# A two-block transformer kernel on one core: halves of square sums folded before TensorE adds them, values computed ahead of transposes, the last layer along rows of tokens, and an earlier first table load

## The chip, the cores and the metric

The kernel runs on 1 core of a Trainium2 chip. The metric is the device time of one execution in microseconds (us). The engines named below are TensorE (PE; PEld is its weight load), VectorE (DVE), ScalarE (ACT), GpSimd (POOL) and SyncE (SP, which here only issues transfers).

## What is computed

256 tokens of width 1024 pass through two blocks, all in float32, with one output of 256 x 1024. Cut to the order of the work:

```
# first block, layer 0: 8 heads of neighbourhood attention + 8 heads of latent attention
x = x + even_mixer(rms_norm(x), ...)          # w_in 1024x1952, w_o 1024x1024
x = x + square(relu(rms_norm(x) @ w1)) @ w2   # 1024x4096, 4096x1024
# layer 1: dilated attention, 3 groups of 16 heads
x = x + odd_mixer(rms_norm(x), ...)           # w_in 1024x9216, w_o 1024x1024
x = x + square(relu(rms_norm(x) @ w1)) @ w2
x = rms_norm(x, norm_final)
# second block: LRU, block attention and attention over a memory, gated and merged
x = x + merged(rms_norm(x)) @ w_out
h = rms_norm(x)
g = causal_dwconv(h @ w_ffn_gate)             # 1024x3072
x = x + (gelu(g) * (h @ w_ffn_up)) @ w_ffn_down   # 3072x1024, "the last layer"
return rms_norm(x, final_norm_gain)
```

## The kernel before

Activations lie transposed: `XT` holds x with features on the partitions, 8 chunks (c) of 128 features by S = 256 tokens. A float32 product is made of three fp32r matmuls: each operand is split into a high and a low part (`XH`/`XL` of the activations, `whi`/`wlo` of the weights, `HH`/`HL` of a hidden layer), and high x high, low x high and high x low are added in PSUM (`product`, L515). Weights come as 192 slabs of at most 1 MB. SP loads slab n into `raw` (5 buffers), ACT makes `whi` (3 buffers, L975), DVE (L1357) or POOL (L2020) makes `wlo`. Each engine calls `ahead(n)` where its program wants slab n + 2 prepared; every engine runs its own program in written order, and waits are on semaphores (`once.wait_ge(*at(event))`). PSUM has 8 banks that TensorE takes in turn (`bank`); a bank is taken again only when its last use is `taken`.

Places that the change touches:

- **Sums of squares for the norms.** ACT squares two chunks at a time into a 128 x 512 tile, DVE or POOL adds the four squares (`add_square`, L1367 and L2031), and `sums` (L572, L576) lets TensorE add over the partitions with a matrix of ones, in true float32: one 256-wide matmul for each half of the tile, and where `cols` is asked for, one 1-wide matmul for each half and each 128 tokens as well. A true float32 matmul leaves two records in the trace.
- **Attention.** `attend(first, n, s)` is step s of a pipeline over heads (u): `scores` of a pair, `transposes` of head s - 2 (L656) and `values` of the pair that ends with head s - 3 (L685). In the first attention (19 steps over 16 heads) other work stands between the steps; in steps 5 to 8 the memory input of the second block is turned (`turn_in`, L587), ACT makes its high part (`memory_high`, L1115) and DVE its low part (`memory_low`, L1623), which also frees the PSUM bank of the turn. DVE's `memory_low(s - 6)` stands behind the whole of `attend`, whose last part is `outputs` (L1458), the low part of the pair's output.
- **Merging of the second block.** On ACT `branch(4)` and `branch(5)` prepare a weight slab each and then wait for merged values (L1271).
- **Last layer.** `down` multiplies with the weights as the stationary operand and 256 tokens as the moving one: 4 column blocks j, 3 slabs each, two halves m, so 576 matmuls of 256 columns. x comes out transposed, is scaled by the gain (`XG`), turned back by TensorE (`rows_out`, L940, 16 transposes), and scaled by the last norm's factor, for which TensorE adds the squares (L958).
- **Start.** SP loads the identity, the first gains, then x in four transfers. TensorE turns x (L587); ACT makes `XH` and `whi` (L1007, L1092); `first_features` (L535) is the first product.

Of the kernel before, what the change touches and what calls it, by code (L numbers as in the profile page):

```python
# [11 lines left out]
P = 128  # L12
S = 256
# [7 lines left out]
        ("ffng", 8), ("fin2", 8), ("qn", 2), ("kvn", 1), ("cw", 16), ("cb", 4), ("ba", 4), ("bx", 4),  # L21
# [104 lines left out]
def weight_plan(A):  # L126
# [67 lines left out]
    down("fd", A["w_ffn_down_2"][0], 24)  # L194
# [81 lines left out]
def build(nc, A, out):  # L276
    with ExitStack() as ctx:
# [21 lines left out]
        with nc.sbuf_tensor("BIG", [P, 16384], F32) as BIG:  # L299
# [35 lines left out]
        s_bias, s_half, s_mem, s_vec, s_roper, s_namask, s_lruw, s_out, s_ident, s_dmask, s_alibi, s_mix = (sem(n) for n in (  # L335
            "s_bias", "s_half", "s_mem", "s_vec", "s_roper", "s_namask", "s_lruw", "s_out", "s_ident", "s_dmask", "s_alibi", "s_mix"))
# [119 lines left out]
        XG, orow = big(14336, 2048, 8), big(6144, 2048, 2)  # L456
# [35 lines left out]
        def tensor(pe):  # L492
# [72 lines left out]
            def sums(name, slot, n=2, cols=False, dilated=False):  # L565
# [179 lines left out]
            def latent_kv():  # L745
# [3 lines left out]
                sums("nq", 1)  # L749

            def rotary_key():
# [4 lines left out]
                sums("nk", 1, n=1)  # L756
# [178 lines left out]
            def rows_out(j):  # L935
                b = bank(("rows", j))
                once.wait_ge(*at(("gained", j)))
                for t in range(2):
                    for c in range(2):
                        m = pe.transpose(b[:, t * S + c * P:t * S + c * P + P], XG[:, 2 * j + c, t * P:(t + 1) * P], ident[:, :])  # L940
                m.then_inc(*tell(s_product, ("product", "rows", j)))

            h = h_ready(2, 24)
            for j in range(4):
                b = [bank(("down", 2, j, m)) for m in range(2)]
                for s in range(3):
                    n = FD + 3 * j + s
                    for m in range(2):
                        event = ("product", "down", 2, j, m) if s == 2 else ("weights", n) if m else None
# [4 lines left out]
            b = bank(("last",))  # L954
            once.wait_ge(*at(("norm", "n7")))
            for t in range(2):
                for c in range(2):
                    m = pe.matmul(b[:, t:t + 1], acc(1)[:, c * S + t * P:c * S + t * P + P], ones[:, 0:1], start=c == 0, stop=c == 1)  # L958
            m.then_inc(*tell(s_product, ("product", "last")))
            rows_out(3)  # L960

        def scalar(act):
# [131 lines left out]

# [237 lines left out]
            for j in range(4):  # L1332
# [7 lines left out]
                if j:  # L1340
                    rows_out(j - 1)
# [897 lines left out]
```

## Time and profile before

| | us |
|---|---|
| median of 3 runs | 1265.96 (1265.52 to 1267.0) |
| profiled execution, its own time | 1267.13 |
| its span, first to last instruction | 1265.3 |
| PE busy | 1245.1 |
| DVE, ACT, POOL busy | 820.8, 618.7, 274.8 |

Busy time of PE includes the time in which a matmul runs through the array, so that PE can be shown as busy while it is issued less often than it could be; the distance between the starts of matmuls is the finer measure. The clock column PEclk is 1.00 at 2.4 GHz and 0.50 at 1.2 GHz.

### The profile page before, as it was taken

How to read it: one execution, taken by the hardware profiler on the slowest of the kernel's cores; microseconds unless marked ns; L12 is line 12 of the kernel's file. 1: busy time of each engine (PE TensorE's matmuls, PEld its weight loads, DVE VectorE, ACT ScalarE, POOL GpSimd, SP SyncE). 2: the span in 40 equal slices, each digit the busy share in tenths (PEclk: the TensorE clock that was granted, in tenths of full speed). 3: DMA queues.
4: the chain of work that ended last, by engine and by line, in shares of the span. 5: the costliest groups of instructions: out<-in, count | busy, mean ns of one | idle time of the engine just before them, and what ended most of it. 6: DMA issues, size and time to landing. Idle time of an engine off the chain costs nothing.

```text
span 1265.3 us, 23972 instructions
## 1 busy us (share of the span) xinstructions
PE 1245.1 (98%) x10309; PEld 1207.0 (95%) x10309; DVE 820.8 (65%) x1106; ACT 618.7 (49%) x765; POOL 274.8 (22%) x205
## 2 busy tenths in 40 slices
PE   7999999999999999999999999999999999999997
PEld 7968899999999999999999999999999999999997
DVE  6768666655565666666877655487876477665653
ACT  5565455544344454545555553345665445444441
POOL 2500010000021202020310000389211595444000
PEclk9999999999999999999999999999999999999998
DMA  9543356555576655464355655555553455555550
GB/s 262 185 134 101 106 170 191 177 189 176 191 225 204 188 170 181 150 191 151 101 166 171 196 171 195 170 172 173 170 165 134 163 170 168 187 180 188 179 167 34
DMA packets 194711, 214.00 MB, mean 169 GB/s; under 512 B 5235, under 2 KB 182718, under 8 KB 194606
## 3 DMA queue, kind: packets, MB, share of 16 engines
q1 hardware_dynamic: 189518, 204.93, 50.3%
q10 hardware_dynamic: 4896, 7.08, 2.0%
q8 instruction: 81, 1.33, 0.5%
q0 software_dynamic: 192, 0.46, 0.1%
q14 instruction: 24, 0.20, 0.1%
HBM read 205.11 MB, written 1.05 MB: 163 GB/s over the span
## 4 chain that ended last, share of the span: by engine, by line
PE 92%; DVE 3%; ACT 2%; POOL 1%; DMA 1%; issue 1%; ACTq 0%; SPq 0%; DVEq 0%; POOLq 0%
PE ps L515 79%; PE ps L648 3%; PE ps L551 3%; PE ps L685 2%; PE ps L656 2%; DVE wlo L1357 1%; PE ps L572 1%; PE ps L535 1%; DVE XL L1391 1%; POOL wlo L2020 1%; DMA TB<-TA 0%; ACT whi L975 0%; ACT SN L1037 0%; ACT XH L1007 0%; ACTq L1195 0%
## 5 line engine op out<-in xcount | busy, mean ns | idle before, releaser
L1357 DVE TENSOR_TENSOR wlo<-raw,whi 128x2048 fp32r<-128x2048 f32 (+1 forms) x155 | 360.1, 2326 | 202.1 <-ACT whi L975 202.0
L515 PE MATMUL ps<-XH,whi 128*128 128x256 f32 x1592 | 451.8, 285 | 0.0
L515 PE MATMUL ps<-XH,wlo 128*128 128x256 f32 x1592 | 448.3, 283 | 0.3 <-DVE wlo L1357 0.3
L515 PE MATMUL ps<-XL,whi 128*128 128x256 f32 x1592 | 448.0, 283 | 0.0
L975 ACT ACTIVATE whi<-raw 128x2048 fp32r<-128x2048 f32 (+1 forms) x189 | 359.5, 1905 | 176.6 <-PE ps L515 154.7
L515 PEld LDWEIGHTS ps<-XH,whi 128*128 128x128 f32 x1592 | 304.3, 192 | 3.2 <-issue 2.9
L515 PEld LDWEIGHTS ps<-XH,wlo 128*128 128x128 f32 x1592 | 304.3, 192 | 0.9 <-DVE wlo L1357 0.8
L515 PEld LDWEIGHTS ps<-XL,whi 128*128 128x128 f32 x1592 | 304.3, 192 | 0.0
L2020 POOL TENSOR_TENSOR wlo<-raw,whi 128x512 fp32r<-128x512 f32 x136 | 180.3, 1358 | 319.5 <-ACT whi L975 319.5
L515 PE MATMUL ps<-HH,whi 128*128 128x256 f32 x832 | 229.5, 283 | 0.0
L515 PE MATMUL ps<-HL,whi 128*128 128x256 f32 x832 | 229.3, 283 | 0.0
L515 PE MATMUL ps<-HH,wlo 128*128 128x256 f32 x800 | 226.5, 283 | 1.0 <-POOL wlo L2020 1.0
L515 PEld LDWEIGHTS ps<-HH,whi 128*128 128x128 f32 x832 | 157.5, 192 | 0.0
L515 PEld LDWEIGHTS ps<-HL,whi 128*128 128x128 f32 x832 | 157.5, 192 | 0.0
L515 PEld LDWEIGHTS ps<-HH,wlo 128*128 128x128 f32 x800 | 153.6, 192 | 1.2 <-POOL wlo L2020 1.2
L2083 POOL TENSOR_TENSOR TB<-TB,BIG 128x512 f32<-128x512 f32 x24 | 42.7, 1781 | 367.4 <-DMA TB<-TA 367.4
L1037 ACT ACTIVATE SN<-SN,stat 128x512 f32<-128x512 f32 (+2 forms) x64 | 38.2, 597 | 102.2 <-DVE stat L1425 93.2
L515 PE MATMUL ps<-whi,XH 128*128 128x256 f32 x256 | 73.2, 286 | 0.0
L515 PE MATMUL ps<-whi,XL 128*128 128x256 f32 x256 | 72.4, 283 | 0.0
L515 PE MATMUL ps<-wlo,XH 128*128 128x256 f32 x256 | 72.4, 283 | 0.0
L515 PE MATMUL ps<-OH,whi 128*128 128x256 f32 x192 | 56.3, 293 | 0.0
L1079 ACT ACTIVATE HH<-TB 128x512 fp32r<-128x512 f32 x32 | 20.2, 632 | 72.7 <-DVE TB L1513 72.7
(229 smaller groups left out, 1604.0 us busy)
## 6 DMA issues: line engine op xcount, KB each, us to landing
raw<-in_mlp_w_dram SPq DMA_DIRECT2D x64, 1024.0 KB, 5.4
raw<-in_od_w_in_dram SPq DMA_DIRECT2D x36, 1024.0 KB, 5.4
raw<-in_w_in_dram SPq DMA_DIRECT2D x24, 1024.0 KB, 5.2
raw<-in_w_ffn_gate_dram SPq DMA_DIRECT2D x12, 1024.0 KB, 5.1
raw<-in_w_ffn_up_dram SPq DMA_DIRECT2D x12, 1024.0 KB, 5.1
raw<-in_w_ffn_down_dram SPq DMA_DIRECT2D x12, 1024.0 KB, 5.0
raw<-in_ev_w_in_dram SPq DMA_DIRECT2D x6, 1024.0 KB, 11.6
TB<-TA ACTq DMA_DIRECT2D x96, 64.0 KB, 4.1
```

The source lines that it names most:

```text
L515: m = pe.matmul(to, l[c][a], r[c][b], start=first and k == 0, stop=last and k == 3 * n - 1)
L535: i = pe.matmul(b[:, m * S:m * S + S], w[m][c][a], x[c][z], start=k == 0, stop=k == len(order) - 1)
L551: i = pe.matmul(b[n][:, m * S:m * S + S], h[a], x[c][z], start=m == c == a == z == 0, stop=m == 1 and c == 7 and z == 1)
L648: m = pe.matmul(banks[u][:, lo:hi], l, r, start=start, stop=stop)
L656: m = pe.transpose(b[:, to:to + P], SN[:, u % 3, of:of + P], ident[:, :])
L685: m = pe.matmul(b[p0:p0 + n, a:z], v, PT[:, u % 3, lo:hi], start=start, stop=stop)
L975: act.activation(whi_of(n), raw_of(n), ACT.Copy, scale=1.0).then_inc(*tell(s_whi, ("whi", n)))
L1037: m = act.activation(SN[:, u % 3, lo:hi], src[:, lo:hi], ACT.Exp, bias=stat[:, u % 3, k:k + 1], scale=-1.0 if biased else 1.0, accum_out=s ...
L1079: act.activation(HH[:, 512 * j:512 * j + 512], TB[j % 2][:, :], ACT.Copy, scale=1.0).then_inc(*tell(s_xhi, ("hhi", layer, j)))
L1357: dve.tensor_tensor(wlo_of(n), raw_of(n), f32(whi_of(n)), ALU.subtract).then_inc(*tell(s_wlo, ("wlo", n)))
L2020: m = pool.tensor_tensor(lo[:, v], r[:, v], f32(hi[:, v]), ALU.subtract)
L2083: pool.tensor_tensor(z, z, twice(RP[:, S:512]), ALU.mult).then_inc(*tell(s_pool, ("sine", k)))
```

## The change

- `sums` gets one half: the adding engine first folds the two halves of the tile (128 x 256 added to 128 x 256), and TensorE runs half the matmuls. For the sums before the last layer (`n6`) the 1-wide ones (`cols`) are added.
- In `attend` on TensorE, `values` stands before `transposes`, and on DVE `memory_low` stands before `outputs`.
- The last layer runs along rows of tokens: HH and HL are the stationary operand (128 features x 128 tokens), and 512 columns of the weights the moving one, 288 matmuls. x is turned to rows beforehand (`rows_in`, 16 transposes among the slabs of the layer before). The square sums then come from ACT's accumulator, along the free dimension. The last gain is loaded as a broadcast row.
- ACT issues the transfers of the identity and the first gains, and runs one Copy at once, which loads its table. TensorE gets 12 matmuls of ones with ones (`keep_busy`), around the turning of x.
- On ACT, the slab of `branch(5)` is prepared before the merged values are waited for.

```diff
@@ weight_plan
-    down("fd", A["w_ffn_down_2"][0], 24)
+    for half in range(2):
+        for k in range(6):
+            add("fd", A["w_ffn_down_2"][0], 4 * k * P, 4, 512 * half, 512)
@@ tensor
-            def sums(name, slot, n=2, cols=False, dilated=False):
+            def sums(name, slot, n=1, cols=False, dilated=False):
@@ attend
+                if 0 <= s - 3 < n and members(group_of(first + s - 3))[-1] == first + s - 3:
+                    values(group_of(first + s - 3))
                 if 0 <= s - 2 < n:
                     transposes(first + s - 2)
-                if 0 <= s - 3 < n and members(group_of(first + s - 3))[-1] == first + s - 3:
-                    values(group_of(first + s - 3))
@@ start
+            def keep_busy(n):
+                once.wait_ge(*at("ones"))
+                for _ in range(n):
+                    pe.matmul(ps[7][:, 0:P], ones[:, :], ones[:, :], start=True, stop=True)
+            keep_busy(3)
             ...
             pe.transpose(b[:, 0:16], rows_[0:16, 2, :], ident[0:16, 0:16])...
+            keep_busy(4)
             for c2 in range(4):
+                if c2 == 2:
+                    keep_busy(2)
                 turn_in(("x", c2), ...)
+            keep_busy(3)
@@ last layer
-            features(FF + 1, x, between=lambda: sums("n6", 0))
+            features(FF + 1, x, between=lambda: sums("n6", 0, cols=True))
             for n in range(FF + 2, FD):
                 features(n, x)
+                if n - FF in (4, 8, 12, 16):
+                    rows_in((n - FF - 4) // 4)
-                        product(b[m][:, 0:S], w_ready(n, 8, m * P, P), h[8 * s:8 * s + 8], event, first=s == 0, last=s == 2)
-                if j:
-                    rows_out(j - 1)
+            for q in range(2):
+                b = [bank(("down", 2, q, t)) for t in range(2)]
+                for k in range(6):
+                    n = FD + 6 * q + k
+                    for t in range(2):
+                        ht = [(HH[:, c * S + t * P:c * S + t * P + P], HL[:, ...], ...) for c in range(4 * k, 4 * k + 4)]
+                        product(b[t][:, :], ht, w_ready(n, 4, 0, 512), event, first=k == 0, last=k == 5)
@@ scalar
+            act.dma_start(ident[:, :], A["c_ident"])...
+            act.dma_start(rows_[0:16, 2, :], A["norm_mix"]...)...
+            once.wait_ge(*at("ones"))
+            act.activation(GG[:, 0:1], ones[:, 0:1], ACT.Copy, scale=1.0)
@@ scalar, last layer
+            def squared_rows(q, t):
+                once.wait_ge(*at(("xr", q, t)))
+                act.activation(..., XR[:, t, 512 * q:512 * q + 512], ACT.Square, accum_out=stat[:, t, q:q + 1])...
+            def row_root(t): ...   # Sqrt of 128 x 1
+            def scaled_row(t, q):
+                once.wait_ge(*at(("root", "n7", t)))
+                once.wait_ge(*at(("yr", q, t)))
+                v = YR[:, t, 512 * q:512 * q + 512]
+                act.activation(v, v, ACT.Copy, scale=r7[:, t:t + 1])...
+            act.dma_start(out[0, P:2 * P, 512:1024], YR[:, 1, 512:1024])...
@@ vector, add_square (gpsimd's alike)
+                if done:
+                    a = acc(slot)
+                    once.wait_ge(*at(("summed", norm, i)))
+                    dve.tensor_tensor(a[:, 0:S], a[:, 0:S], a[:, S:2 * S], ALU.add)...
@@ vector, first attention
-                attend(EVEN, 16, s)
+                attend(EVEN, 16, s, lambda: memory_low(s - 6) if 6 <= s < 10 else None)
-                if 6 <= s < 10:
-                    memory_low(s - 6)
@@ vector, last layer
+            def row_sums(q, t):
+                b = take(("down", 2, q, t), [("taken", "rows", 2 * q + 1)])
+                v = slice(512 * q, 512 * q + 512)
+                dve.scalar_tensor_tensor(out=XR[:, t, v], in0=b[:, :], scalar=r6c[:, t:t + 1], in1=XR[:, t, v], op0=ALU.mult, op1=ALU.add)...
+                dve.tensor_tensor(YR[:, t, v], XR[:, t, v], G2[:, v], ALU.mult)...
+            for t in range(2):
+                row_sums(1, t)
+                row_mean(t)
+                row_scale(t)
@@ sync
-            sp.dma_start(ident[:, :], A["c_ident"])...
-            sp.dma_start(rows_[0:16, 2, :], A["norm_mix"]...)...
```

Three places of the programs are shown as rows, each the instructions of one engine in order. DVE in step 6 of the first attention, from the last maximum (L1425, L1459) on: OL is the output's low part, HL the low part of the memory, SN and PT the probabilities. Before:

```order
L1425 ISA SN,stat<-ps,BIG 128x256
L1425 ISA stat 128x1
L1458 TENSOR_TENSOR OL<-ps,OH 128x256
L1623 SCALAR_TENSOR_TENSOR HL<-ps,V,HL 128x256 x2
L1437 RECIPROCAL stat<-stat 128x2
```

and with the change:

```order
L1459 ISA SN,stat<-ps,BIG 128x256
L1459 ISA stat 128x1
L1657 SCALAR_TENSOR_TENSOR HL<-ps,V,HL 128x256 x2
L1492 TENSOR_TENSOR OL<-ps,OH 128x256
L1471 RECIPROCAL stat<-stat 128x2
```

The low part of the memory now stands ahead of the output's low part, so it no longer waits for ACT's OH; nothing else on DVE has moved here.

TensorE in step 8 of the same attention: scores (L648, L653), the transposes of the probabilities (L656, L661), the values (L685, L690) and the last turn of the memory (MK and MV hold its rows). Before:

```order
L648 MATMUL ps<-BIG 128x256 x8
L656 MATMUL ps<-ident,SN 128x128 x4
L685 MATMUL ps<-PT,BIG 64x256 x4
L587 MATMUL ps<-ident,MK 128x128
L587 MATMUL ps<-ident,MV 128x128
```

and with the change:

```order
L653 MATMUL ps<-BIG 128x256 x8
L690 MATMUL ps<-PT,BIG 64x256 x4
L661 MATMUL ps<-ident,SN 128x128 x4
L592 MATMUL ps<-ident,MK 128x128
L592 MATMUL ps<-ident,MV 128x128
```

The values have moved ahead of the transposes of the next heads; the same happens in every step that has both.

ACT at the end of the merging, in steps 13 and 14 of the third attention: OH is the last head's output, `whi` a weight slab, HH the high part of the merged values. Before:

```order
L1055 ACTIVATE OH<-ps 128x256
L975 ACTIVATE whi<-raw 128x2048
L1271 ACTIVATE HH<-BIG 128x512 x2
L975 ACTIVATE whi<-raw 128x2048
L1271 ACTIVATE HH<-BIG 128x512 x2
```

and with the change:

```order
L1065 ACTIVATE OH<-ps 128x256
L985 ACTIVATE whi<-raw 128x2048 x2
L1285 ACTIVATE HH<-BIG 128x512 x4
L985 ACTIVATE whi<-raw 128x2048 x3
```

The second slab stands ahead of the first two high parts instead of behind them.

## Rows read from the trace of the kernel before

**Rows 1.** The page, busy time: engine, us (share of the span), instructions
```profile
PE 1245.1 (98%) x10309; PEld 1207.0 (95%) x10309; DVE 820.8 (65%) x1106; ACT 618.7 (49%) x765; POOL 274.8 (22%) x205
```

**Rows 2.** TensorE's waits: engine line, whom for, us in total, times, longest
```profile
PE ps L648 <- DVE HL L1623: 2.2, 1, 2.2
PE ps L515 <- POOL wlo L2020: 1.0, 1, 1.0
```

**Rows 3.** Two stretches: length, busy PE, PEld, DVE, ACT, POOL, then PEclk, DMA, GB/s
```profile
87.00:89.40 2.40, 0.23 (x3) 0.00 (x0) 1.23 (x4) 2.40 (x8) 0.00 (x0) 1.00 0.04 14
89.80:96.40 6.60, 6.60 (x28) 2.99 (x24) 4.48 (x13) 2.48 (x9) 0.00 (x0) 0.50 0.01 2
```

**Rows 4.** The first attention in order of time: start, us, engine, line
```profile
84.12 0.60 ACT L991 ACTIVATE SQ<-ps 128x512 f32<-128x512 f32 x1
85.73 0.18 ACT L1037 ACTIVATION_READ_ACCUMULATOR SN<-SN,stat 128x1 f32 x1
...
87.78 0.36 ACT L1055 ACTIVATE OH<-ps 128x256 fp32r<-128x256 f32 x1
88.52 0.87 DVE L1623 SCALAR_TENSOR_TENSOR HL<-ps,V,HL 128x256 fp32r<-128x256 f32 x2
89.44 4.46 PE L648 MATMUL ps<-BIG 64*128 64x256 f32 x16 [2.20 <-DVE HL L1623]
90.75 0.68 DVE L1448 COPY PT<-ps 128x512 f32<-128x512 f32 x1
```

**Rows 5.** TensorE and POOL at the merging's end, in order of time
```profile
1018.80 1.90 ACT L975 ACTIVATE whi<-raw 128x2048 fp32r<-128x2048 f32 x1
1020.84 6.42 POOL L2020 TENSOR_TENSOR wlo<-raw,whi 128x512 fp32r<-128x512 f32 x4 [3.16 <-ACT whi L975]
```

**Rows 6.** The start in order of time
```profile
1.63 1.84 SPq L2152 DMA_DIRECT2D BIG<-in_x_dram  x4
7.14 1.28 ACT L1007 ACT_TABLE_LOAD   x1 [7.14 <-DVE XT L1543]
13.02 1.83 PE L535 MATMUL ps<-XL,whi 128*128 128x256 f32 x8
14.14 1.92 ACT L975 ACTIVATE whi<-raw 128x2048 fp32r<-128x2048 f32 x1 [0.33 <-DMA raw<-in_ev_w_in_dram]
16.60 2.08 PE L535 MATMUL ps<-XH,wlo 128*128 128x256 f32 x16
23.02 2.29 DVE L1357 TENSOR_TENSOR wlo<-raw,whi 128x2048 fp32r<-128x2048 f32 x1 [1.18 <-ACT whi L975]
```

**Rows 7.** Float32 matmuls of 256 and of 512 columns, in order of time
```profile
79.06 1.89 PE L785 MATMUL ps<-BIG 128*128 128x256 f32 x8
80.79 1.88 PE L791 MATMUL ps<-raw,BIG 128*128 128x512 f32 x4
```

**Rows 8.** The sums n4 and n5, in order of time
```profile
826.37 1.02 PE L572 MATMUL ps<-SQ,ones 128*128 128x256 f32 x4
828.04 1.11 PE L572 MATMUL ps<-SQ,ones 128*128 128x256 f32 x4
```

**Rows 9.** The end in order of time
```profile
1254.20 0.60 PE L940 MATMUL ps<-ident,BIG 128*128 128x128 f32 x4
...
1254.40 0.42 DVE L1493 TENSOR_TENSOR TA<-ps,RS 128x256 f32<-128x256 f32 x1 [2.00 <-PE ps L515]
...
1255.32 0.63 ACT L991 ACTIVATE SQ<-XT 128x512 f32<-128x512 f32 x1 [14.79 <-DVE XT L1495]
...
1256.04 0.69 DVE L1367 TENSOR_TENSOR SQ<-SQ 128x512 f32<-128x512 f32 x1 [0.75 <-ACT SQ L991]
...
1258.76 0.20 ACT L1343 ACTIVATE RS<-RS 128x2 f32<-128x2 f32 x1 [2.33 <-DVE RS L1999]
...
1260.02 0.71 ACT L1347 ACTIVATE BIG<-BIG,RS 128x512 f32<-128x512 f32 x1
```

**Rows 10.** The four transfers of the output, from issue to landing
```profile
DMA to landing us min/median/max: 2.1/2.5/2.8
```

More of the change, by code:

```diff
@@ L930, in tensor, with rows_in @@
             features_by_chunks([FF], x)
-            features(FF + 1, x, between=lambda: sums("n6", 0))
+            features(FF + 1, x, between=lambda: sums("n6", 0, cols=True))
+            def rows_in(j):
+                b = bank(("rows", j))
+                for t in range(2):
+                    for c in range(2):
+                        m = pe.transpose(b[:, t * S + c * P:t * S + c * P + P], XT[:, 2 * j + c, t * P:(t + 1) * P], ident[:, :])
+                m.then_inc(*tell(s_product, ("product", "rows", j)))
@@ L954, in tensor @@
[L954 to L960, printed above, removed]
+                if n - FF in (4, 8, 12, 16):
[5 more added lines that the diff above has]
+                    for t in range(2):
+                        event = ("product", "down", 2, q, t) if k == 5 else ("weights", n) if t else None
+                        ht = [(HH[:, c * S + t * P:c * S + t * P + P], HL[:, c * S + t * P:c * S + t * P + P], ("hhi", 2, c // 2),
+                               ("hlo", 2, c // 2)) for c in range(4 * k, 4 * k + 4)]
+                        product(b[t][:, :], ht, w_ready(n, 4, 0, 512), event, first=k == 0, last=k == 5)
+                    released[n] = [event]
@@ L1325, in scalar @@
             ffn_high(11)
-            def rows_out(j):
-                b = take(("rows", j))
-                act.activation(orow[:, :, 256 * j:256 * j + 256], pair(b[:, :]), ACT.Copy, scale=1.0).then_inc(
-                    *tell(s_act_out, ("taken", "rows", j)))
-            for j in range(4):
-                for s in range(3):
-                    ahead(FD + 3 * j + s)
-                once.wait_ge(*at(("xt", "down", 2, j)))
-                if j == 0:
-                    once.wait_ge(*at("ones"))
-                    act.activation(GG[:, 0:1], ones[:, 0:1], ACT.Sqrt)
-                square("n7", 1, j, x0[j], ("xt", "down", 2, j))
-                if j:
-                    rows_out(j - 1)
@@ new lines, in scalar @@
+            for k in range(6):
+                ahead(FD + k)
+            once.wait_ge(*at("ones"))
+            act.activation(GG[:, 0:1], ones[:, 0:1], ACT.Sqrt)
+            for t in range(2):
+                squared_rows(0, t)
+            for k in range(6, 12):
+                ahead(FD + k)
+            for t in range(2):
+                squared_rows(1, t)
+                row_root(t)
+                scaled_row(t, 1)
+            once.wait_ge(*at(("row", 1, 1)))
+            act.dma_start(out[0, P:2 * P, 512:1024], YR[:, 1, 512:1024]).then_inc(*tell(s_out, ("out", 1), by=16))
@@ new lines, in row_mean, with row_scale @@
+            def row_mean(t):
+                once.wait_ge(*at(("rows squared", 1, t)))
+                dve.scalar_tensor_tensor(out=r7[:, t:t + 1], in0=stat[:, t, 1:2], scalar=1.0 / D, in1=stat[:, t, 2:3], op0=ALU.mult,
+                                         op1=ALU.add).then_inc(*tell(s_dve, ("mean", "n7", t)))
+            def row_scale(t):
+                once.wait_ge(*at(("sqrt", "n7", t)))
+                dve.reciprocal(r7[:, t:t + 1], r7[:, t:t + 1]).then_inc(*tell(s_dve, ("root", "n7", t)))
+                once.wait_ge(*at(("root", "n7", t)))
+                once.wait_ge(*at(("yr", 0, t)))
+                dve.tensor_scalar(YR[:, t, 0:512], YR[:, t, 0:512], r7[:, t:t + 1], None, ALU.mult).then_inc(*tell(s_dve, ("row", t, 0)))
@@ new lines, in vector @@
+            for k in range(6):
+                ahead(FD + k)
+            for t in range(2):
+                row_sums(0, t)
+            for t in range(2):
+                once.wait_ge(*at(("rows squared", 0, t)))
+                m = dve.tensor_scalar(stat[:, t, 2:3], stat[:, t, 0:1], 1.0 / D, EPS, ALU.mult, ALU.add)
+            m.then_inc(*tell(s_dve, "rows' first half"))
+            for k in range(6, 12):
+                ahead(FD + k)
+            once.wait_ge(*at("rows' first half"))
```

121 lines of the change are left out of this document (55 added, 66 removed).

## The prediction

> **What bounds the kernel now.** I read the page's busy times first: TensorE is busy for 1245.1 of 1265.3 us, the next engine for two thirds of that [rows 1]. So only two kinds of thing can move the time: TensorE getting less to do or doing it at a shorter distance, and the few places where it waits. The view of its waits names two in the middle, one of 2.2 us in the first attention and one of 1.0 us at the merging's end [rows 2]; the timeline of the start and of the end shows what lies around its work [rows 6, 9]. In the windows I looked for the clock: one stretch of the first attention runs at 0.50 although TensorE is busy all through [rows 3]. Six terms come out of this.
>
> **Term 1, the last layer's matmuls.** 16 fp32r matmuls of 256 columns took 2.08 us [rows 6]. The columns alone are 16 x 256 / 2.4 GHz = 1.71. Eight records of float32 ones of 256 columns took 1.89 and four of 512 took 1.88 [rows 7], so the time goes with the columns alone, at two cycles each: 8 x 256 x 2 / 2.4 GHz is 1.71 as well. So about 0.18 is the last one's way through the array, and the fp32r ones lose a further (2.08 - 1.71 - 0.18) / 15 = 0.013 each: they start 0.120 apart, the float32 ones 0.213 to 0.216. At 1.2 GHz eight fp32r ones of 256 columns took 1.83 [rows 6], and their columns alone are 1.71: nothing lost. The loss thus shows only where a matmul streams for no more than 0.107 us, and is gone in all rows where it streams for 0.213. With 512 columns of fp32r it streams for 0.213, and I take 0.216. 576 x 0.120 = 69.1 becomes 288 x 0.216 = 62.2, a gain of 6.9. The bounds are 0.213 (gain 7.7) and 0.240, where the loss would grow with the columns (gain 0). Against it stand four more turning transposes in TensorE's stream (16 where 12 stood ahead of the last product), at 0.60 for four with the way through the array [rows 9]: 0.4. Net 6.5. DVE's and ACT's work for a slab (2.29 and 1.9 [rows 5, 6]) still fits the 5.2 us of a slab.
>
> The Trainium skill, "TensorE: Matmul & The Clock Gate", section "Back-to-back issue gap", gives columns / 2.4 GHz + 2.5 ns for single matmuls. By that the 512-wide ones would start 0.216 apart, as I take it, and the 256-wide ones 0.109, which the trace contradicts with 0.120. The same section gives some 131 ns at 512 columns for a sustained stream with weight loads; no row here starts wide matmuls faster than their columns stream, and what that would do is a rival below.
>
> **Term 2, the end.** The last product ended at 1254.40, where DVE takes it [rows 9], and the span ends at 1265.3: 10.9. With the change the chain behind the last product is, each with its row's time for the same shape: DVE joins x and the product (0.69 as the 128 x 512 add), ACT squares with its sum (0.63 + 0.18 [rows 4, 9]), DVE a tiny one, ACT's tiny square root (0.20), DVE a tiny reciprocal (0.2 each), ACT scales 128 x 512 (0.71), then the transfer with 2.1 to 2.8 to land [rows 10], I take 2.5. Sum 0.69 + 0.81 + 0.6 + 0.71 + 2.5 = 5.3, and 0.5 for six handovers and for DVE coming late from the rows of the first 128 tokens, whose own chain (about 2.8) is just longer than the 2.6 us (12 x 0.216) of the last product: 5.8. Gain 5.1; bounds 4.5 and 5.6. DVE's multiplication with the gain lies beside ACT's squares.
>
> **Term 3, the first attention.** Before, step 8's scores waited until 89.44 for DVE's L1623 at 88.52, the low part of the memory, which frees their PSUM bank [rows 2, 4]. DVE was late there because it first waited for ACT's OH, done only at 88.14. Its inputs from ACT were ready when the squares ended at 84.72 [rows 4]. With the low part ahead of the output's, it can run at about 86 and the scores start when TensorE arrives, at 87.25. What is late next: the values, which now stand ahead of the transposes, need the probabilities that DVE copies at 90.75 to 91.43 [rows 4]. DVE keeps its order up to there except that 0.87 of work has moved into its wait, so this copy ends about 0.7 earlier, at 90.8. The scores would end at 89.3 at full clock, TensorE waits 1.5, does the values, then the transposes. Second effect: the wait of 2.2 was followed by 6.8 us at 0.50 clock [rows 3], in which the same sixteen scores took 4.46. With scores in the place of the wait and 1.5 as the longest pause, I expect the clock to stay up. That part is then worth 6.8 / 2 = 3.4, and the wait 2.2 - 1.5 = 0.7, less about 0.1 for handovers: gain 4.0. Bounds: 0.6, if the clock falls all the same, and 5.6 if no wait is left. Values ahead of transposes costs nothing elsewhere, since in other steps a slab of 5.8 us lies between a copy of probabilities and its use, and 0.5 here at most; without that slab as cover it costs the wait for one copy, 0.7.
>
> The Trainium skill, same page, section "Part 4: PE-mode transpose", says that transposes do not count as work for the clock. Ahead of the wait here TensorE had run turns and transposes alone, which agrees with a fall after a pause of only 2.2; no row separates the two.
>
> **Term 4, folded sums.** A full set with 1-wide matmuls takes 828.04 - 826.37 = 1.67 [rows 8]; half of it 0.83. The sums mem, n2, n4 and n5 are such: 3.3. n1 and n3 have the 256-wide ones alone, four records of 0.215, half of which is 0.43: 0.9 for both. n6 saves 0.43 and adds as much in 1-wide ones. Gain 4.2; nq and nk keep their work, and n0 is in the next term. The fold itself is a 128 x 256 add on DVE (under 0.69) or POOL, hidden behind the two products that stand ahead of each sum; if it came late, the nearest case is n5, whose add ends 1.5 before its use. Bounds 3.4 and 4.6.
>
> **Term 5, the merging's end.** POOL's slab of 6.42 started at 1020.84, after ACT's `whi` of 1018.80 to 1020.70, and TensorE waited 1.0 for it [rows 2, 5]. ACT can now make this slab when branch 4's product frees the buffer, some 4 us earlier, and POOL starts 3.16 earlier (its idle time). The wait goes. ACT's high parts come 1.9 later, and DVE behind them; the slack of the first is over 2 us. Gain 1.0; bounds 0 and 1.0.
>
> **Term 6, the start.** Four issues take 1.84 [rows 6], so two fewer ahead of x bring all of SP's transfers forward by 0.9. ACT waits for slab 1 at 14.14 and DVE's `wlo` of slab 2 at 23.02 hangs on ACT [rows 6]: this chain moves by 0.9. DVE's idle 1.18 there swallows the fold of n0. TensorE was about a microsecond later than DVE; the folded n0 gives back 0.8 of that. The table load of 1.28 leaves ACT's path, but the weights' transfers bound ACT next. The 12 matmuls of ones lie in waits and raise the clock before 13.02, where it was still low; this too ends at the same transfers. Gain 1.6; bounds 0.9 (transfers alone) and 2.5.
>
> **Sum.** 6.5 + 5.1 + 4.0 + 4.2 + 1.0 + 1.6 = 22.4. The profiled execution took 1267.1 with a span of 1265.3, so its like becomes 1244.7 with a span of 1242.9; the runs' median stands 1.2 below the profiled one, hence 1243.6.
>
> **Rivals.**
> - *All terms hold* (chance 0.60): 1243.6, own range 1241 to 1246.
> - *The clock still falls in the first attention* (0.16). For it: two pauses of 1 to 2 us remain near 89 and transposes stand around them [rows 3, 4]. Against: the pause is shorter and scores fill the old one. 1243.6 + 3.4 = 1247.0.
> - *The loss per matmul grows with the columns* (0.12), 0.240 for 512: 1243.6 + 6.9 = 1250.5. For it: I have no fp32r row of 512 columns. Against: the rows at half clock and in float32.
> - *Waits come back elsewhere* (0.07): a shorter TensorE chain runs into DVE or POOL in the attentions, 3 to 6 us: 1248.
> - *A wide fp32r matmul streams at the float32 rate* of two cycles a column (0.03). This ends on the other side: four float32 ones of 512 take 0.43 each less the way through [rows 7], so 288 x (0.429 - 0.216) = 61.3 more, 1304.9. It decides from 0.216 + 24.9 / 288 = 0.302 per matmul on. Against: weights already move as the 256-wide operand for values without being slower.
> - *Wide matmuls start faster than they stream* (0.01), at 0.131: 288 x 0.085 = 24.5 less, 1219. No row supports it. This is the sustained figure of the Trainium skill's section named in term 1.
> - *The edits do nothing* (0.01): 1266.
>
> A measurement of this kernel can tell about 0.2%, 2.5 us, from no change. Faster: the first four, the sixth, 0.96; same 0.01; slower 0.03. The range leaves out the last three and the edges of the first: 1240 to 1251.
>
> **What the profile would show.** 288 matmuls of 512 columns starting 0.216 apart; a chain of 5.8 us behind the last; no wait of TensorE for L1657 and PEclk 1.00 from 80 to 120; 16 fewer 256-wide records at the sums; no wait for POOL at the merging; DVE's `wlo` of slab 2 at about 22.1. I am wrong in a term if its line is not there, and wrong in the sum by more than 3 us if the last layer's slabs take 5.8 us each or the clock falls near 90.

## The result and the profile after

The changed kernel took 1252.19 us (median of 4 executions, 1251.48 to 1252.65), the kernel before on the same chip 1266.48 (1265.52 to 1267.74): a ratio of 0.9886, interval 0.9869 to 0.9903. That is 14.3 us faster; the prediction took 22.4 off, to 1243.6, and its range began at 1240 and ended at 1251. The direction held, the size did not. The profiled execution has a span of 1250.8, 14.5 less than before.

The page, busy times, as in [rows 1]:
```profile
PE 1232.5 (99%) x10005; PEld 1188.4 (95%) x10005; DVE 819.0 (65%) x1093; ACT 620.3 (50%) x772; POOL 275.0 (22%) x208
```
TensorE still bounds the kernel, with 12.6 us less to do. Its waits that bear on the terms, as in [rows 2] (whom for, us in total, times, longest):
```profile
PE ps L520 <- POOL wlo L2071: 3.7, 2, 2.6
PE ps L690 <- DVE PT L1482: 1.6, 2, 1.3
PE ps L520 <- DVE wlo L1387: 0.5, 1, 0.5
PE ps L653 <- DVE HL L1657: 0.4, 1, 0.4
```
The 2.2 us of [rows 2] for the memory's low part are 0.4 now (L1657), where the prediction had none left, and 1.3 for the copied probabilities (L1482) have come, where it had 1.5. The 1.0 for POOL, which it saw gone, has not gone: there are two such waits, one of 2.6 at the merging's end and one of 1.1 behind the sums n4 and n5.

**The last layer.** Windows inside its products, columns as in [rows 3]; first the changed kernel, then, in a fence of its own, the experiment with halves (below):
```profile
1180.00:1240.00 60.00, 60.00 (x267) 49.66 (x266) 27.08 (x18) 22.54 (x17) 0.00 (x0) 1.00 0.42 140
```
```profile
1184.00:1244.00 60.00, 60.00 (x503) 60.00 (x502) 25.94 (x16) 20.75 (x16) 0.00 (x0) 1.00 0.40 135
```
267 records in 60 us, two of them cut by the edges, are 0.2265 from start to start; over all 288 the mean is 0.2267, the median 0.227. At 256 columns it is 0.120, as before. The columns alone are 0.2133 and 0.1067: at either width about 0.013 is lost. PEld is busy all through with 256 columns and for 49.66 of 60 us with 512, and the loss is the same.

**The first attention**, in order of time (start, us, engine, line), to be held against [rows 4]:
```profile
85.31 0.87 DVE L1657 SCALAR_TENSOR_TENSOR HL<-ps,V,HL 128x256 fp32r<-128x256 f32 x2
86.23 2.60 PE L653 MATMUL ps<-BIG 64*128 64x256 f32 x16 [0.45 <-DVE HL L1657]
89.31 0.68 DVE L1482 COPY PT<-ps 128x512 f32<-128x512 f32 x1
90.14 1.98 PE L690 MATMUL ps<-PT,BIG 128*64 128x256 f32 x8 [1.31 <-DVE PT L1482]
92.05 1.12 PE L661 MATMUL ps<-ident,SN 128*128 128x128 f32 x4
```
and two windows of it:
```profile
87.00:89.40 2.40, 1.83 (x12) 0.77 (x12) 1.80 (x8) 2.40 (x7) 0.00 (x0) 1.00 0.00 0
90.00:93.40 3.40, 3.25 (x15) 2.21 (x16) 2.19 (x6) 1.62 (x5) 0.00 (x0) 0.51 0.00 0
```
VectorE makes the low part at 85.31, the scores behind it take 2.60 where they took 4.46, then the values wait 1.31 for the copy of the probabilities, and behind that the granted clock is at the lower level, for 3.4 us instead of 6.8.

**The merging's end**, where [rows 5] had one wait of 1.0: TensorE, ACT, DVE and POOL in order of time.
```profile
1005.56 1.92 ACT L985 ACTIVATE whi<-raw 128x2048 fp32r<-128x2048 f32 x1 [3.57 <-PE ps L520]
1007.38 0.62 ACT L1285 ACTIVATE HH<-BIG 128x512 fp32r<-128x512 f32 x1
1008.10 1.81 DVE L1932 TENSOR_TENSOR HL<-BIG,HH 128x512 fp32r<-128x512 f32 x1 [2.42 <-ACT HH L1285]
...
1017.84 0.63 ACT L1285 ACTIVATE HH<-BIG 128x512 fp32r<-128x512 f32 x1 [2.16 <-DVE BIG L1928]
1018.38 3.71 ACT L985 ACTIVATE whi<-raw 128x2048 fp32r<-128x2048 f32 x2
1020.42 6.26 POOL L2071 TENSOR_TENSOR wlo<-raw,whi 128x512 fp32r<-128x512 f32 x5 [5.95 <-ACT whi L985]
...
1025.50 0.58 PE L520 MATMUL ps<-HH,wlo 128*128 128x256 f32 x1 [2.58 <-POOL wlo L2071]
```
The slabs from `OUT2` on are those of `w_out`, which TensorE uses right behind the merging. ACT makes the slab `OUT2 + 1` early, as planned, but the slab behind it, `OUT2 + 2`, stands behind ACT's four copies of merged values (L1285), the last of them at 1017.84. Its `whi` comes at 1018.38, POOL has been idle for 5.95 us, and TensorE waits 2.58 for POOL's low part. Behind it the clock falls again:
```profile
1025.30:1028.50 3.20, 3.00 (x14) 3.00 (x15) 0.00 (x0) 0.00 (x0) 3.20 (x4) 0.50 1.03 377
```

**Sums, end, start.** The sums n4 and n5, whose starts were 1.67 apart in [rows 8]:
```profile
818.10 0.59 PE L577 MATMUL ps<-SQ,ones 128*128 128x256 f32 x2
...
818.90 0.68 PE L577 MATMUL ps<-SQ,ones 128*128 128x256 f32 x2
```
0.80 apart now. The end, for [rows 9], from DVE taking the last product at 1244.90 to the last transfer's issue; the span ends 3.0 behind that:
```profile
1244.90 0.75 DVE L2025 SCALAR_TENSOR_TENSOR BIG<-ps,RS,BIG 128x512 f32<-128x512 f32 x1
1245.68 0.63 ACT L1350 ACTIVATE SN<-BIG 128x512 f32<-128x512 f32 x1 [0.55 <-DVE BIG L2025]
...
1247.07 0.72 ACT L1361 ACTIVATE XT<-XT,RS 128x512 f32<-128x512 f32 x1 [0.23 <-DVE RS L2038]
1247.82 0.36 ACTq L1376 DMA_DIRECT2D out_dram<-XT  x1
```
And the start, for [rows 6]:
```profile
0.72 1.81 SPq L2204 DMA_DIRECT2D BIG<-in_x_dram  x4
...
22.47 2.29 DVE L1387 TENSOR_TENSOR wlo<-raw,whi 128x2048 fp32r<-128x2048 f32 x1 [0.72 <-ACT whi L985]
```
The issues are 0.9 earlier, and `wlo` of slab 2 comes at 22.47 instead of 23.02, where 22.1 was forecast.

**Where the time went, stretch by stretch.** The table takes the first matmul of the same piece of work in each trace (of each sum, of each attention's first scores and last values, of the chunks that open a layer) and gives the distance from one to the next, in us. The last row is from DVE's taking of the last product to the end of the span.

| stretch up to | before | after | turns first | merging as before | gates between | no folds | columns, end as before |
|---|---|---|---|---|---|---|---|
| latent queries (start) | 71.62 | 70.42 | 70.59 | 71.06 | 71.08 | 70.72 | 70.91 |
| sum of the memory | 35.98 | 33.53* | 31.17 | 33.44* | 31.98 | 31.98 | 31.98 |
| chunks of the first MLP | 55.68 | 54.34 | 54.88 | 54.34 | 54.48 | 55.22 | 54.41 |
| sum n2 | 190.93 | 190.49 | 190.49 | 190.49 | 190.49 | 190.93 | 190.49 |
| `ODD`'s first scores | 53.68 | 52.80 | 52.80 | 52.80 | 52.80 | 53.68 | 52.80 |
| `ODD`'s last values | 219.36 | 217.24 | 219.49 | 216.83 | 216.82 | 216.82 | 216.85 |
| sum n3 | 19.50 | 19.50 | 19.49 | 19.50 | 19.50 | 19.49 | 19.49 |
| sum n4 | 179.63 | 179.79 | 179.80 | 179.77 | 179.79 | 179.67 | 179.79 |
| gates of the LRU | 32.39 | 31.96 | 31.96 | 31.96 | 31.96 | 32.39 | 31.96 |
| `LAST`'s first scores | 44.43 | 44.43 | 44.43 | 44.43 | 44.43 | 44.43 | 44.43 |
| `LAST`'s last values | 104.70 | 104.25 | 104.70 | 104.25 | 104.25 | 104.25 | 104.25 |
| chunks of slab `FF` (merging) | 36.69 | 39.65* | 39.75* | 36.70 | 35.42 | 38.26 | 39.75* |
| sum n6 | 9.20 | 8.64 | 8.64 | 9.22 | 8.65 | 8.64 | 8.64 |
| DVE takes the last product | 200.63 | 197.88 | 197.78 | 198.01 | 198.03 | 198.56 | 200.75 |
| end of the span | 10.90 | 5.88 | 5.89 | 5.86 | 5.88 | 5.87 | 9.94 |

A star marks a stretch in which the granted clock was at its lower level for 3.4 us; in the kernel before it was there for 6.8 us in the stretch up to the sum of the memory, and in all traces it falls once more near the end. In the first attention one such fall costs 33.5 - 32.0 = 1.5 us, in the merging 39.7 - 38.3 = 1.4. That is less than 3.4 / 2 = 1.7; the last 0.1 to 0.2 of the wait, which lies in the stretch, explains a part of it. These falls come and go between traces with the same wait. Of the seven traces with the change's order of values in step 8 and DVE's low parts early (after, halves, merging as before, gates between, no folds, no ones, columns), three show it behind the wait of 1.3; of the nine with the wait of 2.6 in the merging, eight show it (one of them, with ones in step 8, for 6.8 us). The executions of one kernel differ in the same way: with ones in step 8, two took 1249.8 and 1250.0 at a mean granted clock of 0.999, two 1252.5 and 1252.7 at 0.997. So a median of four carries up to some 1.5 us of this, and single parts are read from the stretches first.

### The profile page after: what moved, and what is told of

Same layout as the page of the kernel before. It is cut to its first block, busy times and chain, and to the rows that moved or that the text cites. A ratio compares the mean times of both kernels' runs of the same rounds, so it can differ in the third digit from the quotient of the medians.

```text
span 1250.8 us, 23346 instructions
## 1 busy us (share of the span) xinstructions
PE 1232.5 (99%) x10005; PEld 1188.4 (95%) x10005; DVE 819.0 (65%) x1093; ACT 620.3 (50%) x772; POOL 275.0 (22%) x208
## 4 chain that ended last, share of the span: by engine, by line
PE 86%; DVE 3%; ACT 2%; issue 1%; POOL 1%; ACTq 0%; DVEq 0%; POOLq 0%
PE ps L520 76%; PE ps L690 2%; PE ps L556 2%; PE ps L653 2%; PE ps L661 2%; ACT whi L985 1%; POOL wlo L2071 1%; DVE wlo L1387 1%; DVE XT L1517 0%; PE ps L890 0%; DVE HL L1932 0%; DVE BIG L1928 0%; DVE XL L1425 0%; ACTq L1210 0%; ACT XH L1017 0%
## 5 line engine op out<-in xcount | busy, mean ns | idle before, releaser
L520 PE MATMUL ps<-HL,whi 128*128 128x256 f32 x640 | 175.6, 284 | 0.0
L520 PE MATMUL ps<-HH,whi 128*128 128x256 f32 x640 | 175.6, 284 | 0.0
L520 PE MATMUL ps<-HH,wlo 128*128 128x256 f32 x608 | 172.9, 284 | 2.6 <-POOL wlo L2071 2.6
L520 PEld LDWEIGHTS ps<-HL,whi 128*128 128x128 f32 x640 | 121.4, 193 | 0.0
L520 PEld LDWEIGHTS ps<-HH,whi 128*128 128x128 f32 x640 | 121.4, 193 | 0.0
L520 PEld LDWEIGHTS ps<-HH,wlo 128*128 128x128 f32 x608 | 117.4, 193 | 2.8 <-POOL wlo L2071 2.8
L1047 ACT ACTIVATE SN<-SN,stat 128x512 f32<-128x512 f32 (+2 forms) x64 | 38.3, 600 | 102.0 <-DVE stat L1459 96.6
## 6 DMA issues: line engine op xcount, KB each, us to landing
raw<-in_ev_w_in_dram SPq DMA_DIRECT2D x6, 1024.0 KB, 11.6
```

Of the source, the lines that this page charges most:

```text
L520: m = pe.matmul(to, l[c][a], r[c][b], start=first and k == 0, stop=last and k == 3 * n - 1)
L1047: m = act.activation(SN[:, u % 3, lo:hi], src[:, lo:hi], ACT.Exp, bias=stat[:, u % 3, k:k + 1], scale=-1.0 if biased else 1.0, accum_out=s ...
```

## The experiments

Twelve kernels, each measured beside the kernel before (whose median was 1266.1 to 1266.6). All but the last two change one thing in the changed kernel. "Theory" and "rival" below are the two outcomes that each expectation names.

**Turns first.** The step of the attention as before:
```
                if 0 <= s - 2 < n:
                    transposes(first + s - 2)
                if 0 <= s - 3 < n and members(group_of(first + s - 3))[-1] == first + s - 3:
                    values(group_of(first + s - 3))
```


> The changed kernel, with one part undone: in the attention's steps TensorE turns the weights (transposes) before it takes the product with the values, as before. Theory (changing between kinds of TensorE work costs about 0.18 us, and values, turns, product has one such change fewer than turns, values, product, with waits at the first attention besides): 2.5 to 4 us slower than the changed kernel, 1254.8 to 1256, most of it in the ODD attention (about 2 us). Rival (the order costs nothing, the ODD attention gained elsewhere): 1252.2.

Measured: 1253.37 (1252.40 to 1253.93), 0.9898 [0.9884, 0.9911]. The median is only 1.2 slower, below what was expected, though the stretches show what was meant: `ODD` takes 219.49, as before, instead of 217.24, `LAST` 104.70 instead of 104.25, the end of the first attention 0.54 more. Against that the stretch up to the memory's sum is 0.8 shorter than the same stretch at full clock elsewhere, 31.17, and has no fall. One step of `ODD`, changed kernel first and this one in the second fence, shows where it lies:
```profile
443.60 1.15 PE L653 MATMUL ps<-BIG 64*128 64x256 f32 x12
444.68 1.09 PE L690 MATMUL ps<-PT,BIG 128*64 128x128 f32 x16
445.70 0.66 PE L661 MATMUL ps<-ident,SN 128*128 128x128 f32 x4
446.12 0.36 PE L520 MATMUL ps<-whi,XH 128*128 128x256 f32 x1
```
```profile
442.05 1.15 PE L653 MATMUL ps<-BIG 64*128 64x256 f32 x12
443.13 0.66 PE L661 MATMUL ps<-ident,SN 128*128 128x128 f32 x4
443.71 1.09 PE L690 MATMUL ps<-PT,BIG 128*64 128x128 f32 x16
444.74 0.39 PE L520 MATMUL ps<-whi,XH 128*128 128x256 f32 x1
```
From the scores to the product behind is 2.52 against 2.69, with the same work and no wait. The transposes take 0.58 of it when values follow and 0.42 when the product follows; values take 1.02 and 1.03. So the order is worth 0.17 in such a group; over all of `ODD` and `LAST` the stretches differ by 2.25 + 0.45 = 2.7 us. It costs 0.8 in the first attention up to the memory's sum, where the values wait 1.3, and gives 0.5 of that back behind it.

**Merging as before, and gates between.** ACT's order at the merging; in the first kernel `branch(4)` stands ahead of `ahead(...("branch", 5))` again. In the second:
```
                        q = 2 * half + j
+                       if q == 1:
+                           ahead(BLENDS + BLEND.index(("branch", 5)))
+                       if q == 3:
+                           ahead(OUT2)
                        once.wait_ge(*at(("merged", q)))
...
-            for k in range(2):
-                ahead(OUT2 + k)
+            ahead(OUT2 + 1)
```
(and no `ahead` of branch 5 in step 14). `ahead(n)` prepares slab n + 2: branch 5 stands for `OUT2 + 1`, `OUT2` for `OUT2 + 2`.

> The changed kernel, with one part undone: at the merging of branches ScalarE's high parts of the next slab stand again behind its gates, as before. Theory (the change moved the wait from slab OUT2+1 to slab OUT2+2, where it is 2.6 us long and lowers the granted clock for 3.4 us): about 3 us faster, 1249, with the wait at OUT2+2 and the stretch at 0.5 gone and a short wait at OUT2+1 back. Rival (the wait at OUT2+2 is from something else, such as GpSimd's low parts): no faster, 1252 to 1253.

> The changed kernel, with ScalarE's order at the merging changed once more: gate 0, high parts of slab OUT2+1, gates 1 and 2, high parts of slab OUT2+2, gate 3. Theory (each slab's high parts ready before TensorE asks, the merged values hardly late): no wait at either slab, about 4 us faster than the changed kernel, 1248. Rival (the merged values come later again and the wait goes on to the slab behind them): 1250 to 1252.

Measured: 1250.33 (1249.00 to 1250.57), 0.9873 [0.9859, 0.9886], and 1247.23 (1247.04 to 1247.35), 0.985 [0.9837, 0.9864]. Merging and the stretch behind it, up to the sum n6, took 45.9 before, 48.3 after, 45.9 with the old order and 44.1 with the one between. The change alone costs 2.4 there, and undoing it gives the 2.4 back. Of the 2.4 some 1.4 is the fall of the clock behind the wait: the trace without folds has the same wait of 2.6 and no fall, and takes 1.4 less. With the gates between, POOL isn't idle at all and TensorE doesn't wait in the window where it waited 2.6 (ACT and POOL, then that window):
```profile
1002.22 24.21 POOL L2073 TENSOR_TENSOR wlo<-raw,whi 128x512 fp32r<-128x512 f32 x16
...
1011.92 1.90 ACT L985 ACTIVATE whi<-raw 128x2048 fp32r<-128x2048 f32 x1
```
```profile
1022.40:1028.40 6.00, 6.00 (x52) 6.00 (x51) 3.15 (x5) 2.62 (x4) 6.00 (x6) 1.00 0.77 264
```
The high part that came at 1018.38 comes at 1011.92. Theory held, rival not. The second is 5.0 us faster than the changed kernel and not 4.2; in its trace the first attention ran at full clock, which gives 1.5, and the start was 0.7 longer.

**Halves.** Each 512-wide product as two of 256 columns in the same orientation:
```
+                        wr = w_ready(n, 4, 0, 512)
+                        for z in range(2):
+                            wz = [(h[:, 256 * z:256 * z + 256], l[:, 256 * z:256 * z + 256], mh, ml) for h, l, mh, ml in wr]
+                            product(b[t][:, 256 * z:256 * z + 256], ht, wz, ...)
```


> The changed kernel, with each 512-wide product of the last layer taken as two products of 256 columns, in the same orientation and over the same operands: 576 instead of 288. Theory (a product of this kind loses a fixed time of about 13 ns whatever its width, 0.2267 from start to start at 512 and 0.120 at 256): 288 x (0.240 - 0.2267) = 3.8 us slower, 1256.0. Rival (the loss grows with the columns, or comes with the orientation: weight loads that take longer beside wider streams): the pair of halves takes as long as the whole, 1252.2.

Measured: 1256.12 (1253.82 to 1258.13), 0.9915 [0.9901, 0.9928], 3.9 slower; from the sum n6 to the last matmul 3.9 more in the trace. That trace has 1.5 more ahead of n6 besides, with a wait of 1.2 for a weight slab's low part that the changed kernel's trace lacks, and the executions spread over 4.3 us; so the stretch carries the reading, and the match of the medians is in part luck. 503 records in 60 us stand above. The loss goes with the number of matmuls, not with columns or orientation.

**Memory behind.** `memory_low(s - 6)` behind the step's outputs on DVE, as before.

> The changed kernel, with one part undone: VectorE's low parts of the memory come behind its outputs of the first attention again, as before. Theory (the first attention's gain rests on them and on the values' order together): 2.5 to 4 us slower, 1254.7 to 1256.2, with a longer wait in the last steps of the first attention. Rival (the order of the values alone makes the gain there): within 0.5 us of 1252.2.

Measured: 1256.37 (1256.13 to 1257.19), 0.9923 [0.991, 0.9935], 4.2 slower, just over what was expected. The stretch up to the memory's sum is 36.63, and two waits of 3.0 and 1.6 for the low part stand in it:
```profile
PE ps L653 <- DVE HL L1657: 3.0, 1, 3.0
PE ps L520 <- DVE HL L1657: 1.6, 1, 1.6
```
DVE's order is the whole of the gain there, and the values' order alone would have made it slower than before (35.98).

**No folds.** `sums` with n=2, and no fold on DVE or POOL.

> The changed kernel, with one part undone: the sums of the norms are taken without folding, as before. Theory (the folds give 4.2 us of TensorE time, of which some 1.6 us were lost again in waits behind the sums n3 and n4/n5, where the producers weren't ready): 2.6 to 4.2 us slower, 1254.8 to 1256.4, and the waits behind n3 and n5 shorter. Rival (all of it was hidden): 1252.2.

Measured: 1253.50 (1252.68 to 1254.42), 0.9899 [0.9886, 0.9913]: 1.3 slower, less than theory. The profiled execution has neither fall of the clock (both stars are missing), which is worth 2.9. By the stretches the folds give 0.88 (memory), 0.44 (n1), 0.88 (n2), 0.43 (n4 and n5) and nothing at n3. At n4 and n5 the two sums together got 1.75 shorter and only 0.43 is left of it, and at n3 nothing is left of 0.43, because the product behind then waits for its weights. Waits between 600 and 900 us of the changed kernel, then of this one (1.1 lies behind n5, 0.5 behind n3):
```profile
PE ps L520 <- POOL wlo L2071: 1.1, 1, 1.1
PE ps L556 <- ACT XH L1017: 0.6, 1, 0.6
PE ps L520 <- DVE wlo L1387: 0.5, 1, 0.5
```
```profile
PE ps L556 <- ACT XH L1017: 0.6, 1, 0.6
```

**No ones; ones in step 8.** `keep_busy` empty; and five filling products of ones in the values' bank ahead of the values of group 2.

> The changed kernel without its filling products of ones (they only keep TensorE busy, their result isn't used). Theory (they cover waits that are there anyway): 0 to 1 us slower, by a stretch at the lower granted clock where they stood. Rival (they are in the way): up to 0.5 us faster.

> The changed kernel, with five filling products of ones (their result isn't used) in step 8 of the first attention, where TensorE waits 1.3 us for the copy of the turned weights and the granted clock then is 0.5 for 3.4 us. Theory (the pause brings the clock down): the clock stays up and 3.4/2 = 1.7 us are gained, 1250.5. Rival (the clock falls for what lay before that pause, the filling changes nothing): 1252.2, with the same 3.4 us at 0.5.

Measured: 1250.42 (1249.90 to 1253.34), 0.9882 [0.9867, 0.9898], and 1251.22 (1249.79 to 1252.65), 0.9881 [0.9868, 0.9895]. Neither tells anything from the changed kernel by its median: both spread over 3 us, with the falls of the clock. Without ones the first product comes earlier, and in this trace it streams at half the pace:
```profile
9.78 2.07 PE L540 MATMUL ps<-XH,whi 128*128 128x256 f32 x8 [1.04 <-ACT whi L1102]
```
With the ones it starts at 10.97 and eight take 1.21. But the other trace without ones, that of the last experiment below, has the full pace too, though TensorE had run nothing but turns ahead of it:
```profile
4.73 3.89 PE L592 MATMUL ps<-ident,BIG 128*128 128x128 f32 x16
9.60 1.21 PE L540 MATMUL ps<-XH,whi 128*128 128x256 f32 x8 [0.99 <-ACT whi L1105]
```
So two traces without ones differ, and that the ones raise the clock isn't shown. The trace with ones in step 8 shows no fall near 90, but so do others without them; whether the filling keeps the clock up stays open.

**Columns and end as before.** All parts but the last layer and the end, which are the code of before (n7 unfolded).

> The changed kernel, with one part undone: the last layer and the end of the program are along columns again, as before (576 products of 256 columns, the output turned and scaled at the end); all other parts stay. Forecast in the prediction: 6.5 for the products and 5.1 for the end, 11.6 us slower, 1263.8. Theory (the traces of this study: 200.4 against 197.8 us from the sum n6 to the last product, 10.9 against 6.0 us behind it): 7.5 us slower, 1259.7.

Measured: 1258.27 (1257.77 to 1260.55), 0.9939 [0.9926, 0.9953]: 6.1 slower than the changed kernel, not 11.6. Theory's 7.5 was nearer. The trace has 200.75 and 9.94 where the changed kernel has 197.88 and 5.88, 6.9 more, against which the clock stays up in its first attention (1.5 less). Its end is 9.94 and not the 10.90 of before, with the same instructions. The eight tiny sums at its heart show why, before first, then here:
```profile
1256.88 1.66 PE L958 MATMUL ps<-ones,SQ 128*128 128x1 f32 x8 [2.08 <-DVE SQ L1367]
```
```profile
1248.96 1.02 PE L969 MATMUL ps<-ones,SQ 128*128 128x1 f32 x8 [2.07 <-DVE SQ L1384]
```
In the trace of before the clock fell 0.2 us behind the start of the first of them, here it fell behind them. So of the 5.0 that term 2 gained in the profiles about 0.9 is that chance, and at equal clock the end is worth 4.1.

**Turns first in step 8, and together.** `transposes` ahead of `values` for `first == EVEN and s == 8` alone; the same with the gates between; and both without ones.

> The changed kernel, with the transposes ahead of the values in one step alone, step 8 of the first attention, where the values wait 1.3 us for VectorE's copy of turned weights. Theory (the step's transposes fill 0.5 us of that wait, which is then too short for the granted clock to fall): 31.2 instead of 32.0 us from the latent queries to the sum of the memory, no stretch at 0.5 near 90, and 0.8 to 1.6 us faster, 1251. Rival (the transposes are late in any order, the wait only moves to them): 1252.2.

> The changed kernel with two edits together: ScalarE's order at the merging (gate 0, slab OUT2+1, gates 1 and 2, slab OUT2+2, gate 3), which alone measured 1247.2, and the transposes ahead of the values in step 8 of the first attention. Theory (they are independent): 0.8 us less than the first alone, 1246.4. Rival (the granted clock stays up in the first attention of that kernel in most executions anyway, or what is gained there is waited for behind it): 1247.2.

> The same two edits, and without the filling products of ones at the start (their result isn't used). Theory (the first product comes 1.3 us earlier without them, at 9.8 instead of 11.1, though the clock rises later, and 0.6 us of it is left at the latent queries): 0.6 us less than with them, 1245.8. Rival (what was measured without them, 1250.4 against 1252.2, was the chance of the clock in the merging): 1246.4 or up to 0.5 us more.

Measured: 1250.80 (1249.97 to 1251.51), 0.9877 [0.9863, 0.989]; 1247.01 (1246.91 to 1247.29), 0.9848 [0.9834, 0.9861]; 1246.87 (1246.27 to 1247.33), 0.9846 [0.9832, 0.9859]. The first takes 31.65 up to the memory's sum and 54.74 behind it, together 86.4. That is what the gates between (86.5) and the columns (86.4) took with the values first and the clock up, so none of the 0.8 is left. The values' wait there is 0.7 instead of 1.3. What the median gained, 1.4, is as much as one fall of the clock costs, and the clock stayed up near 90 in all four traces that turn first in step 8. Together with the gates between it adds 0.2, within what can't be told: the rival. The ones at the start are worth nothing that could be measured: without them 0.14 less, though the trace without them has a fall of 3.4 us at 25.4, behind a wait of 1.6 for weights. The best two kernels beat both kernels of this case, by 19.6 and 5.2 us for the one with ones.

## Why the prediction was wrong

| term | forecast | in the traces | from |
|---|---|---|---|
| 1, last layer's products | 6.5 | 2.8 | 200.63 - 197.88, n6's sum with it |
| 2, end | 5.1 | 5.0 | 10.90 - 5.88; 4.1 at equal clock |
| 3, first attention | 4.0 | 2.5 | 35.98 - 33.53; 4.0 with the clock up |
| 4, folds | 4.2 | 2.5 | 0.88 + 0.44 + 0.88 - 0.16 + 0.43 |
| 5, merging | 1.0 | -2.4 | 45.9 - 48.3 |
| 6, start | 1.6 | 1.2 | 71.62 - 70.42; 0.5 to 1.0 in the other five |
| not forecast: order of values | 0 | 3.0 | 2.12 in `ODD`, 0.45 in `LAST`, 0.46 behind the first attention |
| sum | 22.4 | 14.5 | span 1265.3 - 1250.8 |

**Term 1 is mis-sized.** The prediction argued that the loss per matmul "is gone in all rows where it streams for 0.213" and took 0.216. It isn't gone: 0.2267 for 512 columns, 0.120 for 256, hence 0.013 for each fp32r matmul at full clock, and the halves cost 3.9 where 288 x 0.0133 is 3.8. The gain is 288 x (0.240 - 0.2267) = 3.8 instead of 6.9. The rows that it went by were of another kind, float32 at two cycles a column and fp32r at the lower clock; neither is a wide fp32r matmul at full clock. The rival beside it, a loss that grows with the columns, was wrong as well: truth lay in the middle of the two, a constant loss, which was the plainest reading of the one row at hand. The Trainium skill, "TensorE: Matmul & The Clock Gate", section "Back-to-back issue gap", gives 2.5 ns on top of the columns for single matmuls; this trace has 13 at both widths. Of the turning transposes 0.4 was booked. A stop of TensorE for four of them costs 0.44: from the last product ahead to the second one behind it is 0.68, where two steps of 0.12 would be 0.24. Four such stops stand where two stood, 0.9 more. 3.8 - 0.9 is 2.9, where 2.8 was measured; n6's sum is as long as before (0.98 and 1.00 to the second product behind it).

**Term 2** held by its chain, 5.88 where 5.8 was forecast. Its 10.9 of before was read as the cost of that end; about 0.9 of it was the lower clock in that execution, so that the gain came out so near to 5.1 is in part luck.

**Term 3**: the chain came as forecast, to within 0.5 us. Put back by the 1.2 of the earlier start, the low part ran at 86.5 for 86 and the scores began at 87.4 for 87.25, after a wait of 0.4 where none was forecast; the values waited 1.31 for 1.5. "I expect the clock to stay up" failed in this execution and held in others: at full clock the stretch is 31.98, exactly 4.0 less than before. It was the second rival, with 0.16; the traces make it three in seven, at 1.5 us and not 3.4. The prediction also lets transposes not count as work for the clock. The two rows of turns and first product above speak against that: the clock was up behind sixteen turns and one small transpose alone. And ahead of the wait in the kernel before, TensorE had run turns and transposes alone for 1.5 us only, behind scores and values.

**Term 4**: the folds shortened TensorE's sums by what was forecast, and "hidden behind the two products that stand ahead of each sum" is right for the fold itself. What failed is that a shorter TensorE chain meets what the other engines have ready at that point. Behind n3 and behind n5 TensorE comes earlier and then waits 0.5 and 1.1 for low parts. The rival "waits come back elsewhere" named this, but in the attentions.

**Term 5 is the step that failed by its reasoning.** "ACT can now make this slab ... The wait goes. ACT's high parts come 1.9 later ... the slack of the first is over 2 us." It looked at the slab moved forward and at the products that read the merged values, not at the next slab in ACT's own queue. That slab stands behind all four copies of merged values, each of which waits for DVE, which waits for the copy ahead of it. POOL, which the change was to serve, was idle for 5.95 us instead of 3.16. Bounds of 0 and 1.0 held no loss at all. Instead of 1.0 gained, 2.4 was lost: about 1.0 by the longer wait and 1.4 by the clock behind it. Both kernels that alter only this order show it.

**Term 6** was near: DVE's `wlo` of slab 2 came 0.55 earlier and not 0.9, and the stretch 1.2 shorter, in the other five traces of the table 0.5 to 1.0. What it says of the ones isn't borne out: without them the time is the same.

**The order of values** was costed at nothing, "Values ahead of transposes costs nothing elsewhere", with waits as the only price looked for. TensorE loses 0.17 more in a group when transposes stand ahead of values than ahead of a product. That is a price of its own, beside the waits. The gain of 3.0 was luck as far as the prediction goes. Undoing the order alone measured only 1.2 slower, since the values' wait in the first attention is then 0.4 instead of 1.3, and no fall of the clock follows it in that trace.

The six terms were forecast at 22.4 and brought 11.5. The misses are 3.7, 0.1, 1.5, 1.7, 3.4 and 0.4, 10.9 before rounding, and the unforecast gain takes 3.0 back: 7.9 us. The measured median is 8.6 above the forecast. The other 0.7 is that the prediction let the median stand 1.2 below the profiled execution, and it stands 0.4 below it now.

## What to carry to other kernels

When a chunk of work is moved forward on an in-order engine, follow the item behind it as well as the moved one: here the wait went to the next slab and grew from 1.0 to 2.6. A gain on the bounding engine is only kept up to the point where its suppliers are ready, so each place where it arrives earlier needs its suppliers' times. A constant loss per matmul seen at one width is to be taken as constant at another until a row of the same type and clock says otherwise; and changes of kind in TensorE's stream (scores, transposes, values, products) have prices that can be read off the trace of before.

## What was not expected of the hardware

- An fp32r matmul starts 0.013 us later than its columns at full clock, for 256 and for 512 columns alike, with weight loads of 0.19 beside it; with 512 columns the loads leave 17% of the time free and the loss stays.
- Four transposes cost 0.58 us ahead of the values and 0.42 ahead of an fp32r product, with no wait in the trace.
- The granted clock after a pause is no function of the pause that the trace shows: behind the same 1.3 us it fell in three of seven traces, behind the same 2.6 us in eight of nine, and one fall of 3.4 us costs about 1.5 us. Executions of one kernel that differ in it differ by up to 3 us in time, which hides single effects of that size.
- The clock at the start differs between traces as well. Without ones the first eight products took 2.07 us in one trace and 1.21 in the other, behind the same sixteen turns.
